# Cached pages as records that hold both layouts, a ring of seven record groups, and half of the requests on ScalarE

## The reference

```python
past_c = cache_ckv[page_table].reshape(DB, past_len, KV_LORA)
past_pe = cache_kpe[page_table].reshape(DB, past_len, ROPE_DIM)
...
s = (jnp.einsum('bqhc,bkc->bhqk', ql, kc) + jnp.einsum('bqhr,bkr->bhqk', qp, kpe)).astype(jnp.float32) * scale
s = jnp.where(k_pos[None, None, None, :] <= pos[None, None, :, None], s, -jnp.inf)
p = jax.nn.softmax(s, axis=-1).astype(kc.dtype)
return jnp.einsum('bqhk,bkc->bqhc', p, kc)
```

## Time and profile before

| | |
|---|---|
| median of 3 executions | 1430.48 us (1430.45 to 1430.55) |
| span of the profiled execution, first to last instruction | 1428.4 us |
| median less that span | 2.1 us |
| TensorE busy | 1412.2 us, 99% of the span |
| VectorE, ScalarE, POOL busy | 889.8, 742.7 and 161.9 us |
| granted TensorE clock | 0.999 |
| scores of unit 0 begin, values of unit 15 begin | 1023.54 and 1140.32 us |

### The profile page before, as it was taken

One profiled execution on the slowest core, in us unless ns is written; L12 is line 12 of the kernel. 1 busy time (PEld: TensorE's weight loads), 2 busy tenths in 40 slices (PEclk: granted clock), 3 DMA queues, 4 the chain that ended last, 5 costly groups with the idle time before them and its releaser, 6 DMA issues.

```text
span 1428.4 us, 29450 instructions
## 1 busy us (share of the span) xinstructions
PE 1412.2 (99%) x11003; PEld 1346.2 (94%) x11003; DVE 889.8 (62%) x1480; ACT 742.7 (52%) x1218; POOL 161.9 (11%) x229
## 2 busy tenths in 40 slices
PE   9999999999999999999999999999999999999998
PEld 9999999999888999999999999999877699999998
DVE  6655535999888675554376555349755548655534
ACT  6555424788646565553265555346533346555423
POOL 0111000010110011110011111001144201111000
PEclk9999999999999999999999999999999999999999
DMA  6444443344242254444434444444599643444441
GB/s 242 163 149 151 153 154 136 119 152 146 100 155 98 89 177 147 147 147 148 147 119 166 154 151 147 154 147 150 187 293 285 212 156 118 169 152 150 147 147 67
DMA packets 50776, 221.01 MB, mean 155 GB/s; under 512 B 6705, under 2 KB 23474, under 8 KB 28802
## 3 DMA queue, kind: packets, MB, share of 16 engines
q1 hardware_dynamic: 38882, 189.07, 38.0%
q0 software_dynamic: 6192, 24.64, 5.2%
q10 hardware_dynamic: 5616, 6.16, 1.3%
HBM read 213.07 MB, written 6.77 MB: 154 GB/s over the span
## 4 chain that ended last, share of the span: by engine, by line
PE 94%; DVE 3%; ACT 2%; issue 1%; DMA 0%; DVEq 0%
PE psum L283 16%; PE psum L287 15%; PE psum L282 15%; PE psum L381 8%; PE psum L380 8%; PE psum L382 8%; PE psum L2681 2%; PE psum L2639 2%; PE psum L309 1%; PE psum L300 1%; PE psum L325 1%; PE psum L304 1%; PE psum L2510 1%; PE psum L311 1%; PE psum L315 1%; PE psum L1553 1%
## 5 line engine op out<-in xcount | busy, mean ns | idle before, releaser
L270 DVE TENSOR_TENSOR w_lo<-raw,w_hi 128x2048 fp32r<-128x2048 f32 x159 | 368.6, 2318 | 290.5 <-ACT w_hi L263 290.4
L263 ACT ACTIVATE w_hi<-raw 128x2048 fp32r<-128x2048 f32 x155 | 296.7, 1914 | 351.7 <-PE psum L382 207.8
L282 PE MATMUL psum<-h_hi,w_hi 128*128 128x320 f32 x1504 | 446.0, 310 | 0.0
L283 PE MATMUL psum<-h_lo,w_hi 128*128 128x320 f32 x1504 | 444.1, 309 | 0.0
L282 PEld LDWEIGHTS psum<-h_hi,w_hi 128*128 128x128 f32 x1504 | 282.1, 188 | 2.6 <-issue 1.3
L283 PEld LDWEIGHTS psum<-h_lo,w_hi 128*128 128x128 f32 x1504 | 283.4, 188 | 0.5
L287 PE MATMUL psum<-h_hi,w_lo 128*128 128x320 f32 x1504 | 251.3, 309 | 0.0
L287 PEld LDWEIGHTS psum<-h_hi,w_lo 128*128 128x128 f32 x1504 | 228.3, 188 | 0.3 <-DVE w_lo L270 0.3
L380 PE MATMUL psum<-hid_hi,w_hi 128*128 (+1 forms) x704 | 217.4, 309 | 0.0
L381 PE MATMUL psum<-hid_lo,w_hi 128*128 (+1 forms) x704 | 217.4, 309 | 0.0
L382 PE MATMUL psum<-hid_hi,w_lo 128*128 (+1 forms) x704 | 217.4, 309 | 0.0
(11 more groups left out here) (459 smaller groups left out, 1957.4 us busy)
## 6 DMA issues: line engine op xcount, KB each, us to landing
raw<-wts SPq DMA_DIRECT2D x161, 1024.0 KB, 4.8
h_plain<-cache_t POOLq DMA_DIRECT2D x44, 160.0 KB, 3.7
h_plain<-cache_t SPq DMA_DIRECT2D x44, 160.0 KB, 3.7
arena<-s POOLq DMA_DIRECT2D x4, 1024.0 KB, 7.2
sgs<-arena POOLq DMA_DIRECT2D x4, 1024.0 KB, 4.6
marena<-cache_t POOLq DMA_DIRECT2D x20, 160.0 KB, 4.0
marena<-cache_t SPq DMA_DIRECT2D x20, 160.0 KB, 3.6
raw<-cache_c SPq DMA_DIRECT2D x16, 128.0 KB, 4.2
```

Source lines behind the costliest of these rows:

```text
L263: act.activation(w_hi[c0 % 2][:, :], raw_of(c0, pair)[:, :], ACT.Copy).then_inc(hi_ready, 1)
L270: eng.tensor_tensor(w_lo[c0 % 2][:, :], raw_of(c0, pair)[:, :], w_hi[c0 % 2][:, :].bitcast(F32), ALU.subtract).then_inc(lo_ready, 1)
L282: pe.matmul(outs[n], wtile(w_hi, c0, tile0 + n * K + k), src_hi(k), start=(k == 0), stop=False)
L283: pe.matmul(outs[n], wtile(w_hi, c0, tile0 + n * K + k), src_lo(k), start=False, stop=False)
```

## The change

A page becomes one record, `cache_tc`: 128 partitions of 576 values, the channel layout and rotary key first (320), the token layout behind it (256), 288 KB. One request brings all of it. A group is the four records of one sample in one unit, so a unit has two groups, 2i and 2i+1, and seven group buffers form a ring: two in `h_plain`, two in `marena`, three in a new `page_pool` that lies over four weight buffers. `page_plain_pe`, `copy_plain`, `load_pages`, `load_first_plain` and `load_plain` go; `load_records` comes. SP requests all groups of the first samples; POOL those of the second samples for units 0 and 1; ScalarE those of the second samples for units 2 to 15, four requests at a time, ahead of its round. Small buffers (`qpk`, `pts`, `ptn`, `osb`) move, and the chunk behind the attention (`uk` + 2) is requested after the values of unit 13 instead of unit 14.

```diff
-        NTS = 3
+        REC = PGW + KV_LORA
+        GW = QP * REC
+        NTS, NGB = 3, 7
...
+        gbuf = [a_.rearrange("p (g n) -> p g n", g=QP) for a_ in
+                [h_plain[:, i * GW:(i + 1) * GW] for i in range(2)]
+                + [marena[:, o_ + i * GW:o_ + (i + 1) * GW] for i in range(2)]
+                + [page_pool[:, free0 + i * GW:free0 + (i + 1) * GW] for i in range(3)]]
...
+        def records(i, s):
+            return gbuf[(2 * i + s) % NGB]
...
             pe.wait_ge(aland[i % NTS], 16 + 16 * QP * (i // NTS + 1))
-            pe.wait_ge(bland[i % NTS], 16 * QP * (i // NTS + 1))
+            if i < 2:
+                pe.wait_ge(bland[i], 16 * QP)
+            else:
+                pe.wait_ge(cland[i % NTS], 16 + 16 * QP * ((i - 2) // NTS + 1))
...
-        def page_plain_pe(pe, i):
-            if i:
-                pe.wait_ge(c_dve, i)
-            for g in range(2):
-                for w in range(2):
-                    o = (2 * g + w) * P
-                    last = pe.transpose(bank[C_BANK[0]][:, o:o + P], slot[i % NTS][:, g, 0, w * P:(w + 1) * P], ident)
-            last.then_inc(c_tr, 1)
...
-                    last = pe.matmul(bank[V_BANK][rows, 0:KV_LORA], pts[:, g, rows], plain_b[i % 2][g] if s else first_plain(i, g),
+                    last = pe.matmul(bank[V_BANK][rows, 0:KV_LORA], pts[:, g, rows], records(i, s)[:, g, PGW:REC],
...
             pack_act(act)
-            load_first_plain(act, 0)
+            load_records(act, 1, cland, 2)
             for n in range(NUN):
+                if 2 <= n < NUN - 1:
+                    load_records(act, 1, cland, n + 1)
...
-                if n < NUN - 1:
-                    load_first_plain(act, n + 1)
...
+        def load_records(eng, s, land, i):
             p, q = i // NQT, i % NQT
+            j = 2 * i + s
+            if j >= NGB:
+                eng.wait_ge(pv_page, QP * ((j - NGB) // 2 + 1))
+            elif j >= 4:
+                eng.wait_ge(chunk_done, BASE["uk"] + 1)
+                eng.wait_ge(lo_ready, BASE["uk"] + 2)
             for g in range(QP):
                 n = page_of(eng, 2 * p + s, QP * q + g)
+                eng.dma_start(records(i, s)[:, g, :], io["cache_tc"][bass.ds(n, 1), :, :].rearrange("a p n -> p (a n)")) \
                    .then_inc(land[i % NTS], 16)
...
+            for i in range(1, NUN):
+                load_records(sp, 0, aland, i)
+            sp.wait_ge(pv_page, QP * (NUN - 2))
+            load_chunk(sp, BASE["uk"] + 2)
             sp.wait_ge(n_scores, NP)
             sp.wait_ge(s_done, NUN)
-            sp.wait_ge(pv_page, QP * (NUN - 1))
-            load_chunk(sp, BASE["uk"] + 2)
```

More of the change, by code:

```diff
@@ L132, in sem @@
             return ctx.enter_context(nc.semaphore(name))
-        raw = [sb(f"raw{i}", [P, CHUNK]) for i in range(2)]
-        w_hi = [sb(f"w_hi{i}", [P, CHUNK], F32R) for i in range(2)]
-        w_lo = [sb(f"w_lo{i}", [P, CHUNK], F32R) for i in range(2)]
+        RT = BASE["uk"] % 2
+        s0 = ExitStack()
+        in_pool = [(f"raw{1 - RT}", F32), (f"raw{RT}", F32), (f"w_hi{RT}", F32R), (f"w_lo{RT}", F32R)]
+        wbuf = {name: sb(name, [P, CHUNK], dt, s0) for name, dt in in_pool}
+        s0.close()
+        page_pool = sb("page_pool", [P, 4 * CHUNK])
+        wbuf |= {name: sb(name, [P, CHUNK], F32R) for name in (f"w_hi{1 - RT}", f"w_lo{1 - RT}")}
+        raw, w_hi, w_lo = ([wbuf[f"{kind}{i}"] for i in range(2)] for kind in ("raw", "w_hi", "w_lo"))
         con = sb("con", [P, CW])
@@ L2230, in build @@
[L2230 to L2236, removed]
@@ L2237, in build @@
-        o_ += CW_
-        qpe = marena[:, o_:o_ + HEADS // 2 * TOK].rearrange("p (h t) -> p h t", h=HEADS // 2)
[L2239 to L2246, removed]
+        qd = marena[:, o_ + 3840:o_ + 3840 + 4 * TOK].rearrange("p (t n) -> p t n", t=4)
@@ new lines, in build @@
+        qpe = marena[:, o_:o_ + HEADS // 2 * TOK].rearrange("p (h t) -> p h t", h=HEADS // 2)
+        o_ += HEADS // 2 * TOK
+        qpk = [a_.rearrange("p (b q) -> p b q", b=NP) for a_ in
+               (page_pool[:, 0:NP * P], page_pool[:, NP * P:Q01], marena[:, o_:o_ + NP * P])]
+        ptn = marena[0:NSMP, o_ + NP * P:o_ + 2 * NP * P].rearrange("p (b q) -> p b q", b=NP)
+        assert o_ + 2 * NP * P <= AW - H2 - 2 * 2 * HEADS * TOK
+        osb = page_pool[:, Q01:free0]
+        pts = h_plain[:, 2 * GW:2 * GW + QP * P].rearrange("p (g q) -> p g q", g=QP)
@@ L2256, in build @@
         nst = lambda j, p=0, n=1: lnv[:, 128 + 4 * j + p:128 + 4 * j + p + n]
-        aland, spland = first_landed[0], first_landed[1][0:2]
+        aland, cland = first_landed[0], first_landed[1]
         bland = [sem(f"bland{i}") for i in range(NTS)]
-        ppland = [sem(f"ppland{i}") for i in range(2)]
         (dq_taken, dq_sq, dq_n, qn_hi, qn_lo, qp_taken, qp_rot, qp_step, qpe_ready, uk_done,
@@ L2628, in scores_pe @@
             p = i // NQT
-            t = slot[i % NTS]
+            t = [records(i, s) for s in range(2)]
             pe.wait_ge(aland[i % NTS], 16 + 16 * QP * (i // NTS + 1))
-            pe.wait_ge(bland[i % NTS], 16 * QP * (i // NTS + 1))
+            if i < 2:
+                pe.wait_ge(bland[i], 16 * QP)
+            else:
+                pe.wait_ge(cland[i % NTS], 16 + 16 * QP * ((i - 2) // NTS + 1))
             if i >= 1:
@@ L2638, in scores_pe @@
                     for s in range(2):
-                        pe.matmul(o[s][f], qpk[:, w, p, s * NSMP:(s + 1) * NSMP],
-                                  t[:, :, s, w * P + f * HP:w * P + (f + 1) * HP], start=(w == 0), stop=False)
+                        pe.matmul(o[s][f], qpk[w][:, p, s * NSMP:(s + 1) * NSMP],
+                                  t[s][:, :, w * P + f * HP:w * P + (f + 1) * HP], start=(w == 0), stop=False)
             for s, f in ((0, 0), (1, 1), (0, 1), (1, 0)):
                 rows = slice(f * ROPE, (f + 1) * ROPE)
-                last = pe.matmul(o[s][f], qpk[rows, 2, p, s * NSMP:(s + 1) * NSMP], t[rows, :, s, 2 * P:PGW],
+                last = pe.matmul(o[s][f], qpk[2][rows, p, s * NSMP:(s + 1) * NSMP], t[s][rows, :, 2 * P:PGW],
                                  start=False, stop=True)
@@ L2746, in transposed @@
                 act.wait_ge(s_tr, i + 1)
-                act.wait_ge(pv_page, QP * i) if i else act.wait_ge(lo_ready, BASE["uk"] + 2)
+                if i:
+                    act.wait_ge(pv_page, QP * i)
                 act.activation(pts, bank[T_BANK][:, :].rearrange("p (g q) -> p g q", g=QP), ACT.Copy).then_inc(s_trt, 1)
@@ L3071, in _ @@
             pack_pool(pool)
[L3072 to L3075, removed]
-            for i in range(NUN - 2, NUN):
-                load_plain(pool, 1, ppland, i)
             second_high_pool(pool, BASE["ffn3"] + 1)
```

88 lines of the change are left out of this document (19 added, 69 removed).

## The result

The changed kernel takes **1452.05 us** (median of 4 executions, 1450.64 to 1456.66) against 1430.51 beside it: ratio 1.0155 (1.0138 to 1.0171), **21.5 us slower**. Forecast was +11.9. The direction, the place and the mechanism came out as predicted; the size did not, and the value lies just outside the range. The four executions have mean granted clocks of 0.995, 0.997, 0.997 and 0.999, the slowest the lowest. The profile is of the slowest of them, 26.6 us longer in its span than the profile before.

What follows compares the result with a forecast made beforehand. TensorE, busy 1412.2 of 1428.4 us, was taken as the bound, with DMA nearly full. Rounds of 8.32 against 7.405 us, times 13, give +11.9, ends 0: 1430.5 + 11.9 = 1442.4 us, range 1435 to 1452.

Steps and rivals of the forecast that it cites:

- what goes: TensorE's page transposes in the attention: pipelined, so removing them saves 0.44 us a round, 6.2 us in 14 rounds.
- ScalarE's requests: Four requests ahead of ScalarE's copies delay them: mean round 7.96 us against 7.405, a loss of 0.55 per round.
- The spacing of 1.06: Time in us between ScalarE's successive requests, mostly the page number's fetch; the fourth would end 4.41 into the round.
- the copy at 4.46 into the round: ScalarE's copy of the numerators, needed at 3.11 us into the round, would start at about 4.46 behind four requests.
- the two-round sum: Landing 9.5 plus TensorE's work 7.135 us make two rounds: 8.32 each, 0.91 over 7.405, +11.9 us in 13 rounds.
- eight records together: One release lets SP and ScalarE request eight records together; the four needed first get half the DMA engines.
- So ScalarE's group is there at 0.71 + 1.7 + 7.08 = 9.5 us after the release.: Landing after unit's last values: first request 0.71, fixed latency 1.7, eight records at 333 GB/s 7.08 us.
- Only the requests bind: Rival: at 370 GB/s or more landing is by 8.79 us, rounds 7.96, +7.2, 1437.7 us; chance 0.17.
- Two of the signs: Expected in the changed profile's attention stage: DMA share about 0.85 to 0.95, records landing near 4 to 5 us.
- DMA stays as it is: Rival: DMA engines deliver 285 GB/s, landing at 10.7, rounds 8.91 us, +19.6, 1450.1 us; chance 0.12.
- the ends: Round 0's late exponential against units 0 and 1's saved transposes: 0 taken, between -0.9 and +1.3 us.

Runs made afterwards that it cites:

- e4: The kernel before the change with one of each unit's four page transposes, the other three left out (stale data); 1426.16 us, 0.9973.
- e2: The changed kernel with the second samples' record requests issued by POOL instead of ScalarE, SP unchanged; 1456.46 us, 1.0183.
- e1: The changed kernel with SP's requests for units 4 to 15 held back until the round's scores are done; 1443.68 us, 1.0096.
- e7: The changed kernel with SP and POOL each requesting two records of the needed group, then two of the later one, ScalarE none; 1432.88 us, 1.0018.
- e11: e9 with each record's rows padded in memory to 2560 B; 1430.95 us, 1.0003.
- e3: The changed kernel with POOL requesting the second samples' groups and SP's requests held back until the round's scores are done; 1454.35 us, 1.0163.
- e9: e7 with each record requested when its own buffer's values are done, not the whole unit's; 1431.58 us, 1.0008.

## Why the prediction was right in kind and short in size

**Right: what goes.** "A round saves 0.44 us": e4 gives 4.0 us for three quarters of the transposes.

**Right: ScalarE's requests, and that the landing hides them.** The spacing of 1.06 and the copy at 4.46 into the round came out within 0.2 us (the 0.05 from ScalarE to TensorE in that sum stands in no row; the earlier trace rows give 0.09), and the long waits stand ahead of the scores in odd rounds, as the two-round sum has it. They come to 17.2 us in 13 rounds, 1.3 a round, where about 1.2 were expected. e2 takes the requests off ScalarE and gains nothing.

**Right: eight records together.** Three comparisons show it. In the changed kernel itself unit 15's group, asked for alone, lands after 7.2 us instead of 10.4. In e1 the order alone changes, and where the hold is long the group lands after 7.4 to 8.7 us. e7 changes order and engines of the requests and not their bytes, and the time returns to 0.2% above the kernel before. e7 by itself doesn't separate the order from splitting the needed group over two engines and taking ScalarE's requests away; the other two do. e2, with POOL in ScalarE's place and the old order, gains nothing. The rule of the Trainium skill that the prediction named (DMA: Bandwidth & Descriptors, "Issuing engines are not separate DMA queues") agrees: e2 moves the urgent records to another engine's queue and the waiting scores still start 1047.58 - 1037.05 = 10.53 and 1066.28 - 1056.03 = 10.25 us after the release.

**Wrong: "So ScalarE's group is there at 0.71 + 1.7 + 7.08 = 9.5 us after the release."** It is there after 10.64. This term of the sum was mis-sized. The landing of unit 5's group in three pieces, from the release to the scores (columns as above):

```profile
1060.08:1062.50 2.42, 2.42 (x26) 1.25 (x23) 0.88 (x4) 0.00 (x0) 0.00 (x0) 1.00 0.23 16
1062.50:1068.00 5.50, 5.25 (x33) 3.24 (x32) 3.06 (x11) 2.48 (x8) 0.00 (x0) 1.00 0.98 363
1068.00:1070.46 2.46, 0.00 (x0) 0.03 (x1) 1.28 (x5) 0.00 (x0) 0.00 (x0) 1.00 0.61 178
```

The start is as the sum has it: 0.71 + 1.7 us in which almost nothing arrives. In the middle the engines are full and deliver 363 GB/s, more than the 333 of the sum and nearly the 370 of the rival "Only the requests bind". What the sum lacks is the end: I divided the bytes by one rate as if the engines were full to the last byte, and they are at 0.61 and 178 GB/s for the last 2.5 us. Units 9 and 11 show the same (182 and 156 GB/s for the last 2.7 and 2.2 us). So 332 over the whole stretch meets 333 as the mean of a faster middle and a slower end. Why the last packets are late stays open; e11 laid the rows further apart in memory and changed nothing. Two of the signs failed with this term: the DMA share is 0.61 to 0.75 instead of 0.85 to 0.95, and records land after 5.3 us in the median instead of 4 to 5. The rival "DMA stays as it is" took the delivered rate, 285 GB/s, and had landing at 10.7 and 1450.1 us; its reason, a lower rate throughout, was not the true one, and that its numbers came close is luck. In the 13 rounds there are six such landings (unit 15's group goes alone): 6 x 1.14 = 6.8 us.

**Missing: a term for the clock.** The earlier trace rows showed a full clock with TensorE never idle, and I carried that over. In the profiled execution the granted clock falls to 0.50, the lower of its two levels (1.2 GHz), for 3.4 us three times in the stage (1052.6, 1090.1 and 1144.7), each time about 1.1 us after scores had resumed behind a wait. From these scores to the next release the rounds of units 3, 7 and 13 take 8.7, 8.6 and 8.7 us; in e1, without a fall, they take 7.1, 7.1 and 7.3. That is about 1.5 us each, 4.4 together. The falls are not in every execution to this extent: the one with mean clock 0.999 took 1450.64, still 20 us above the kernel before, so the landing is the larger part.

Put together for the 13 rounds of the profile: 11.9 + 6.8 + 4.4 = 23.1, measured 23.7; the 0.6 were not followed up. In the median, with the executions that have a higher mean clock, +21.5.

**Right: the ends.** Round 0 and 1 gave +0.3 (0 taken, -0.9 to +1.3), the end 0.0.

## What to carry to other kernels

When one release lets two engines ask for data, list what each asks for in the order in which it is needed: here the same bytes in the order of need, with the needed group split over two engines, took 1432.9 us, and in two queues side by side 1452. Size a landing by the delivered rate of a burst, from the request to the last packet, not by the rate at full share: here 242 against 332 GB/s. And before adding bytes to a stage whose DMA engines are at 0.95, compare their price with the gain: here 2.36 for 2.10 MB cost about 3 us, against some 5.3 us for the transposes that they replace.

## What was not expected of the hardware

POOL's requests go out in fewer, larger packets than SP's for the same records. The queues of e9 from 1040 to 1130 us (packets, MB, share of 16 engines' time):

```profile
q1 hardware_dynamic: 6862, 14.06, 51.0%
q0 software_dynamic: 3836, 14.15, 41.6%
```

That is 2.05 KB against 3.69 KB on average, and less engine time for the same bytes. In the trace POOL's data packets are 4608 B, two rows of a record, and SP's 2304 B, one row. Whether this is worth time was not tried.

The falls of the clock did not follow from the length of a wait alone. In the changed kernel's profile waits of 3.42, 2.73 and 2.21 us (units 3, 7 and 13) have a fall of 3.4 us about 1.1 us after their end, and waits of 2.56, 2.81 and 2.18 us (units 5, 9 and 11) have none. In e2 and e3 some falls begin before the wait has ended, and some last 6.8 us. The first of e2 begins 0.7 us before the scores at 1047.58:

```profile
1046.89:1050.30 3.41, 2.72 (x14) 1.81 (x16) 0.00 (x0) 0.00 (x0) 1.11 (x3) 0.50 0.86 285
```
